# Layer 0's first squares summed on VectorE, pieces of the weight splits moved, and two expert tiles begun 64 bytes later

## The reference

```python
def rmsnorm(t, g):
    tf = t.astype(jnp.float32)
    y = tf * lax.rsqrt(jnp.mean(tf * tf, axis=-1, keepdims=True) + EPS) * g.astype(jnp.float32)
    return y.astype(t.dtype)
...
    rq = axial_rotary(heads(xs[4], RET_HEADS).astype(f32), *rope)
    rk = axial_rotary(heads(xs[5], RET_HEADS).astype(f32), *rope) * HEAD_DIM ** -0.5
...
    for e in range(N_EXPERTS):
        out = out + combine[:, e:e + 1].astype(t.dtype) * swiglu(t, w_gate[e], w_up[e], w_down[e])
```

## Time and profile before

| | |
|---|---|
| median of 3 runs | 2854.11 us (2850.2 to 2856.61) |
| the profiled execution | 2855.72 us, of which its span is 2853.9 us (1.8 us lie around it) |
| mean granted TensorE clock | 0.959 of 2.4 GHz |
| busy: PE, PEld | 2691.5 us (94%), 2267.1 us (79%) |
| busy: DVE, ACT | 1815.8 us (64%), 1462.7 us (51%) |
| chain that ended last | PE 85%, DVE 8%, ACT 4%, issue 2%, DMA 1% |
| experts | about from 1830 to 2829 us of the span |

### The profile page before, as it was taken

One profiled execution on the slowest core, in us unless ns is written; L12 is line 12 of the kernel. 1 busy time (PEld: TensorE's weight loads), 2 busy tenths in 40 slices (PEclk: granted clock), 3 DMA queues, 4 the chain that ended last, 5 costly groups with the idle time before them and its releaser, 6 DMA issues.

```text
span 2853.9 us, 38902 instructions
## 1 busy us (share of the span) xinstructions
PE 2691.5 (94%) x15426; PEld 2267.1 (79%) x15426; DVE 1815.8 (64%) x1907; ACT 1462.7 (51%) x1624; POOL 29.8 (1%) x40
## 2 busy tenths in 40 slices
PE   6999889999898999889899998899999999999998
PEld 3875568888796899877789986788888888888887
DVE  3224655553535676673355554688888888888887
ACT  3226333332335455532144444577777777777775
POOL 0001000000002000000000000000000000000000
PEclk8999999999999999996899999899999999999998
DMA  7546412322231444320034441599999999999996
GB/s 292 195 164 261 181 59 89 117 78 109 81 126 52 182 167 154 148 89 1 1 136 180 172 153 60 213 362 339 364 344 339 367 340 362 344 364 343 344 357 245
DMA packets 84359, 590.43 MB, mean 207 GB/s; under 512 B 9616, under 2 KB 10000, under 8 KB 19472
## 3 DMA queue, kind: packets, MB, share of 16 engines
q1 hardware_dynamic: 82800, 576.79, 54.5%
q10 hardware_dynamic: 1440, 11.93, 1.1%
HBM read 587.63 MB, written 1.05 MB: 206 GB/s over the span
## 4 chain that ended last, share of the span: by engine, by line
PE 85%; DVE 8%; ACT 4%; issue 2%; DMA 1%; DVEq 0%; POOL 0%; ACTq 0%; SPq 0%; POOLq 0%
PE banks L469 23%; PE banks L470 22%; PE banks L471 22%; PE banks L475 16%; DVE ring_rounded L531 2%; ACT ring_rounded L521 1%; DMA ring<-in_stream 1%; PE banks L2860 1%; PE banks L906 1%; DVE rstd L815 0%; ACT scratch L983 0%; DVE aT L2257 0%; DVE activations L1418 0%; DVE nmax L949 0%; DVE hT L1583 0%
## 5 line engine op out<-in xcount | busy, mean ns | idle before, releaser
L531 DVE TENSOR_TENSOR ring_rounded<-ring,ring_rounded 128x2048 fp32r<-128x2048 f32 (+4 forms) x168 | 339.6, 2023 | 455.1 <-ACT ring_rounded L521 454.1
L470 PE MATMUL banks<-aT_rounded,ring_rounded 128*128 128x256 f32 (+1 forms) x1632 | 532.0, 326 | 0.0
L470 PE MATMUL banks<-ring_rounded,activations_rounded 128*128 128x512 f32 x1344 | 527.5, 392 | 0.0
L521 ACT ACTIVATE ring_rounded<-ring 128x2048 fp32r<-128x2048 f32 (+4 forms) x168 | 284.7, 1696 | 395.1 <-PE banks L471 386.7
L469 PE MATMUL banks<-aT_rounded,ring_rounded 128*128 128x256 f32 (+2 forms) x1120 | 338.3, 302 | 24.6 <-DVE aT_rounded L840 12.5
L470 PEld LDWEIGHTS banks<-aT_rounded,ring_rounded 128*128 128x128 f32 x1632 | 317.4, 195 | 24.3 <-issue 0.7
L471 PE MATMUL banks<-aT_rounded,ring_rounded 128*128 128x256 f32 (+2 forms) x1120 | 335.7, 300 | 0.0
L470 PEld LDWEIGHTS banks<-ring_rounded,activations_rounded 128*128 128x128 f32 x1344 | 252.7, 188 | 52.3
L3034 DVE TENSOR_TENSOR ring_rounded<-ring,tables_rounded 128x2048 fp32r<-128x2048 f32 x112 | 253.4, 2286 | 24.1 <-ACT tables_rounded L2952 23.9
L2952 ACT ACTIVATE tables_rounded<-ring 128x2048 fp32r<-128x2048 f32 x112 | 214.9, 1920 | 94.4 <-DMA ring<-in_stream 88.8
L469 PE MATMUL banks<-activations_rounded,ring_rounded 128*128 128x512 f32 (+1 forms) x724 | 247.9, 342 | 14.8 <-DVE aT_rounded L845 7.1
(11 more groups left out here) (333 smaller groups left out, 4796.5 us busy)
## 6 DMA issues: line engine op xcount, KB each, us to landing
ring<-in_stream SPq DMA_DIRECT2D x501, 1024.0 KB, 5.4
ring<-in_stream SPq DMA_DIRECT2D x32, 704.0 KB, 5.4
ring<-in_stream SPq DMA_DIRECT2D x28, 768.0 KB, 6.1
activations<-in_rpb ACTq DMA_DIRECT2D x2, 1536.0 KB, 6.3
ring<-in_stream SPq DMA_DIRECT2D x6, 512.0 KB, 5.1
tables<-in_tab_b ACTq DMA_DIRECT2D x1, 2436.0 KB, 8.6
tables<-in_tab_a ACTq DMA_DIRECT2D x1, 2304.0 KB, 9.0
hT<-in_h ACTq DMA_DIRECT2D x1, 2048.0 KB, 15.7
```

The lines of the kernel that those rows point to most:

```text
L470: pe.matmul(out, exact(upper), exact(w_lower), start=False, stop=False)
L521: act.activation(exact(upper), w, ACT.Copy).then_inc(g.s["act_pieces"], 1)
L531: dve.tensor_tensor(exact(w), w, rounded(upper), ALU.subtract).then_inc(g.s["dve_pieces"], 1)
```

## The change

It has five parts.

1. Start: norm ("n1", 0) is gathered on DVE like the others (blocks 1 to 6), and PE sums only blocks 6 and 7. ACT copies modulation rows 1 before it takes the root (`then`), and rows 2 and 3 before it issues the late tables.
2. Splits at the start: one piece is split ahead of the first norm and one within it, instead of two ahead.
3. The rotary on DVE stands before the last weight piece of the projection, in both layers (`rotate_first_dve`).
4. Layer 0 after retention: ACT makes one weight piece before the last block of the attended values. In norm ("n2", 0) the gathers stand behind the additions, PE sums from block 5 on, and the DVE's weight piece of m = 6 goes behind m = 7. In norm ("n1", 1) ACT's weight piece moves from the end to before the third square.
5. The two expert tiles in `tables` begin 16 floats (64 bytes) later.

```diff
 def first_sum(key):
-    if key in (("n1", 0), "last"):
+    if key == "last":
         return 0
-    return KD - 3 if key in (("n1", 1), ("n2", 1), "ffn0", "ffn1") else KD - 2
+    return KD - 3 if key in (("n1", 1), ("n2", 0), ("n2", 1), "ffn0", "ffn1") else KD - 2
 def is_gathered(key):
-    return key not in (("n1", 0), "last")
+    return key != "last"
...
     upper_act(g, act, end)
+    then()
     act.wait_ge(g.s["pe_norm"], g.at("summed", key, KD - 1))
...
 def proj_dve(g, dve, l):
     dve.wait_ge(g.const_in["tab_a"], 16)
     for name in IN_ORDER:
+        if name == IN_ORDER[-1]:
+            rotate_first_dve(g, dve, l)
         lower_dve(g, dve, 1 if name in (IN_ORDER[0], IN_ORDER[-1]) else 2)
...
-    for name in ("rq", "rk"):
-        for j in range(3):
...
     if l == 0:
+        upper_act(g, act, 1)
         out_upper_act(g, act, 7)
-        upper_act(g, act, 2)
+        upper_act(g, act, 1)
...
-... g.tabs[:, 1536:1536 + UNIT], g.tabs[:, 3584:3584 + UNIT],
+... g.tabs[:, 1552:1552 + UNIT], g.tabs[:, 3600:3600 + UNIT],
...
-        squares_act(g, e, ("n1", 0), g.hT, T2, None)
+        squares_act(g, e, ("n1", 0), g.hT, T2, None, then=lambda: mod_act(g, e, 0, 1))
+        for i in range(2, MOD_FIRST):
+            mod_act(g, e, 0, i)
         consts_act(g, e, False)
-        for i in range(1, MOD_FIRST):
-            mod_act(g, e, 0, i)
...
+        for k in range(1, KD - 1):
+            gather_dve(g, e, ("n1", 0), T2, k)
         rstd_dve(g, e, ("n1", 0), T2)
...
             if l == 0:
-                upper_act(g, e, 2)
+                upper_act(g, e, 1)
             e.wait_ge(*g.moment(("gain", l, 0)))
-            split_act(g, e, n1, T2, lambda k, s: g.mod[:, l, k, s:s + 1], g.n1_upper, l)
+            split_act(g, e, n1, T2, lambda k, s: g.mod[:, l, k, s:s + 1], g.n1_upper, 1)
...
         if l == 0:
-            only("dve", add_dve, "wo", l, T, lambda m, s: g.mod[:, l, 16 + m, s:s + 1], n2, lambda m: {0: 2, 6: 1}.get(m, 0))
+            only("dve", add_dve, "wo", l, T, lambda m, s: g.mod[:, l, 16 + m, s:s + 1], n2, lambda m: 2 * int(m == 0),
+                 lambda m: int(m == KD - 1), False)
...
-            squares_act(g, e, after, g.hT, T, lambda k: ("free", ("dn", l, k)), split_ahead_1 if l else lambda k: 0, 1 - l)
+            squares_act(g, e, after, g.hT, T, lambda k: ("free", ("dn", l, k)), split_ahead_1 if l else lambda k: int(k == 2))
```

More of the change, by code:

```diff
@@ L675, in first_sum, with squares_act @@
 def first_sum(key):
-    if key in (("n1", 0), "last"):
+    if key == "last":
         return 0
-    return KD - 3 if key in (("n1", 1), ("n2", 1), "ffn0", "ffn1") else KD - 2
+    return KD - 3 if key in (("n1", 1), ("n2", 0), ("n2", 1), "ffn0", "ffn1") else KD - 2
 def is_gathered(key):
-    return key not in (("n1", 0), "last")
-def squares_act(g, act, key, src, T, ready, pieces=lambda k: 0, end=0):
+    return key != "last"
+def squares_act(g, act, key, src, T, ready, pieces=lambda k: 0, end=0, then=lambda: None):
     for k in range(KD):
@@ L1067, in proj_act, with rotate_first_dve @@
             mod_act(g, act, l, MOD_FIRST + IN_ORDER.index(name))
+def rotate_first_dve(g, dve, l):
+    for name in ("rq", "rk"):
+        for j in range(3):
+            x = g.m1[name][:, j, 0:L]
+            dve.wait_ge(g.s["pe_projection"], g.at("mm", "swap", name, l, j))
+            dve.tensor_tensor(g.tmp[:, 4096:4096 + L], g.bank(("swap", name, l, j))[:, 0:L], g.tab("rot_sin"), ALU.mult).then_inc(g.s["dve_projection"], 1)
+            g.count("dve_projection", ("free", ("swap", name, l, j)))
+            dve.tensor_tensor(x, x, g.tab("rot_cos"), ALU.mult).then_inc(g.s["dve_projection"], 1)
+            g.count("dve_projection")
+            dve.wait_ge(g.s["dve_projection"], g.so_far("dve_projection"))
+            dve.tensor_tensor(x, x, g.tmp[:, 4096:4096 + L], ALU.add).then_inc(g.s["dve_projection"], 1)
+            g.count("dve_projection", ("rotated", name, l, j))
+            dve.wait_ge(g.s["dve_projection"], g.so_far("dve_projection"))
 def proj_dve(g, dve, l):
@@ L1815, in second_places @@
     g.units = [flat[:, UNIT * i:UNIT * i + UNIT] for i in range(EXPERT_RING)]
-    g.upper = [flat[:, UNIT * EXPERT_RING:UNIT * EXPERT_RING + UNIT], g.tabs[:, 1536:1536 + UNIT], g.tabs[:, 3584:3584 + UNIT],
+    g.upper = [flat[:, UNIT * EXPERT_RING:UNIT * EXPERT_RING + UNIT], g.tabs[:, 1552:1552 + UNIT], g.tabs[:, 3600:3600 + UNIT],
                wide[:, 0:UNIT], wide[:, UNIT:2 * UNIT], t[:, 2560:2560 + UNIT]]
@@ L3324, in first_block @@
             if l == 0:
-                upper_act(g, e, 2)
+                upper_act(g, e, 1)
             e.wait_ge(*g.moment(("gain", l, 0)))
-            split_act(g, e, n1, T2, lambda k, s: g.mod[:, l, k, s:s + 1], g.n1_upper, l)
+            split_act(g, e, n1, T2, lambda k, s: g.mod[:, l, k, s:s + 1], g.n1_upper, 1)
         if kind == "dve":
             if l == 0:
-                lower_dve(g, e, 2)
+                lower_dve(g, e, 1)
             e.wait_ge(*g.moment(("gain", l, 0)))
             norm_dve(g, e, n1, g.hT, T2, lambda k, s: g.gain[:, l, 0, k, s:s + 1], lambda k, s: g.mod[:, l, k, s:s + 1],
-                     None, g.n1_upper, l)
+                     None, g.n1_upper, 1)
         only("act", bias_act, l)
```

## The result

The changed kernel took **2821.57 us** (median of 4 runs, 2821.16 to 2823.66), the kernel before 2855.36 (4 runs, 2850.2 to 2858.29) beside it: a ratio of 0.9888, 95% interval 0.9876 to 0.99, or 34 us less. A second series gave 2825.19 (5 runs, 2821.01 to 2832.36) against 2852.35 (18 runs), a ratio of 0.991 (0.9895 to 0.9926), or 27 us less. The forecast was 2829, from a sum of 26.4 us, with a range of 2821 to 2840. Both medians lie in the range. The sum was nearer to the second series than to the first, and the experiments show why: up to 13 us of these kernels' time hang on the moments at which the granted clock falls, and no part of the change was made to set those.

What follows compares the result with a forecast made beforehand. PE was taken as the bound nearly everywhere, so only shortening its idle or slow time counted. Terms 6.7 + 6.3 - 1.2 + 3.7 + 0.8 + 10.1 = 26.4 us, off 2855.7, gave 2829 us, range 2821 to 2840.

Steps and rivals of the forecast that it cites:

- start: From kernel start to first projection matmul: fewer PE sums, shorter waits and a moved weight piece save 6.7 us, bounds 4 and 9.5.
- rotary, layer 0: End of layer 0's projection: rotating before the weight piece removes PE's 4.59 us wait and low clock, saving 6.3 us.
- rotary, layer 1: Layer 1's gate: PE waits for the weight piece until 863.0, losing 1.2 us; bounds 0 and 3.
- ("n2", 0): Layer 0's second norm: reordered gathers, additions and weight piece bring the reciprocal earlier, saving 3.7 us; bounds 2 and 4.
- ("n1", 1): Layer 1's first norm: moving ACT's piece lets the reciprocal follow the root directly, saving 0.8 us; bounds 0 and 0.8.
- expert tiles: In the experts, starting the two `tables` tiles 64 bytes later makes their units fast, saving 10.1 us; bounds 0 and 12.3.
- only the root: Start, behind the sums: PE no longer waits for the copy of modulation rows 1, only the root; 0.75 us less.
- The piece: Start, last modulation sum to first projection matmul: one DVE piece moves into the norm, saving 0.7 us.
- Rival 3: Start gives nothing: modulation runs at 1.2 GHz without the sums beside it and gathers are late; 2836 us, chance 0.05.
- ACT's early piece: In layer 0's retention: saves nothing, as PE's next wait is for the second piece.
- Rival 1: Experts: the tiles' start doesn't matter, the two are slow for another reason; 2839 us, chance 0.11.
- H1: Experts, later theory from the forecast's reading: moving-to-stationary distance modulo 512 counts, 256 is slow; test should save some 5 us.

Runs made afterwards that it cites:

- part4_only: Kernel before with part 4 alone (norms ("n2", 0) and ("n1", 1), ACT's early piece in the retention): 2849.85 us, ratio 0.9987.
- start_only: Kernel before with parts 1 and 2 alone (first norm gathered on DVE, one weight piece ahead of it): 2842.83 us, ratio 0.9956.
- again: The changed kernel run once more, nothing altered, in a second series: five runs, 2821.01 to 2832.36 us, median 2825.19.
- rotary_l0: Changed kernel with the rotary ahead of the last weight piece in layer 0 only, layer 1 in its old order: 2821.75 us.
- tiles_only: Kernel before with part 5 alone (the two expert tiles in `tables` 64 bytes later): 2842.95 us, ratio 0.9964.
- mixed_l1: Changed kernel with layer 1's query tiles rotated ahead of the last weight piece, key tiles behind it: 2836.71 us, in a second series 2838.0.
- sweep_a: Changed kernel with expert tiles in `tables` at 464 and 576 bytes beyond a multiple of 1024, `scratch` meant at 448; no time clearly given.
- sweep_b: Changed kernel with expert tiles in `tables` at 480 and 960 bytes beyond a multiple of 1024, `scratch` meant at 192; no time clearly given.
- starts_c: A kernel whose change and time the text given does not state under this name.
- stationary_64: Changed kernel with the experts' stationary tiles (xg, hT2) 64 bytes later: 2855.08 us, beside the changed kernel's 2825.19.

## Why the prediction was right, point by point

| term of the sum | predicted | shown | by |
|---|---|---|---|
| start | 6.7 | 10.4 at the first projection matmul (8.3 against part4_only's old start) | changed, start_only |
| rotary, layer 0 | 6.3 | 6.3 (130 to 200) | changed, again, rotary_l0 |
| rotary, layer 1 | -1.2 | -3.2 | changed against rotary_l0 |
| ("n2", 0) | 3.7 | 3.6 at the reciprocal | part4_only, changed, again |
| ("n1", 1) | 0.8 | 0.7 | the same |
| expert tiles | 10.1 | 10.4 | tiles_only |
| changes of expert | 0 | 2.1 (0.5 and 1.8 with the old tiles: start_only, part4_only) | changed |
| the clock elsewhere | 0 | about 4, and 1 in the other profile | changed, again |

*Start: the term was mis-sized, at a step of its own.* The end of the two sums at 25.5 (25.35) and the wait for "only the root" (0.7 less) were right. "Bounds: 4 (the modulation runs at the low clock throughout, as it has less PE work beside it) and 9.5 (at the high clock throughout)": the condition of the upper one came true (the clock was 1.00 throughout the modulation), the term went 0.9 us beyond it, and I had taken the middle by leaving the modulation as it was. The row 34.40 to 41.20 is the 2.9 us. The piece gave 1.3, not 0.7, because the issue of the two transfers ran beside ACT's last copy instead of behind it, as ACT's timeline shows:

```profile
32.78 0.60 ACT L637 ACTIVATE mod_rows<-banks 128x512 f32<-128x512 f32 x1 [3.03 <-PE banks L475]
32.79 0.35 ACTq L500 DMA_DIRECT2D tables<-in_tab_a  x1
33.18 0.45 ACTq L500 DMA_DIRECT2D pool_w<-in_pool_w  x1
33.67 1.48 ACT L521 ACTIVATE ring_rounded<-ring 128x1536 fp32r<-128x1536 f32 x1 [0.29 <-issue]
```

The first projection matmul was forecast near 43.5 and came at 39.8. Rival 3, the opposite of this, was wrong by its premise that fewer sums leave the clock low: after the sums, the clock next falls at 36 to 40 us in all ten profiles with the new start, behind the modulation, and in all four with the old one at 33 to 34.5, within it.

*Rotary, layer 0.* Right in size. Its "bounds 3 and 6.3" held; 1.5 us of it went again by 230 us, because the clock was at 0.50 for 6.8 us (204.1 to 210.9) where the kernel before had 3.4 (225.5 to 228.9).

*Rotary, layer 1.* The wait was forecast as one for the piece, of 2 to 3 us, and was 2.89 us. "1.2 us lost; bounds 0 and 3 (a low clock after the wait)": the wait cost 1.3 us, about as summed, and the clock, which I had left to the bound, the rest: with it the term went 0.2 beyond the bound. After 2.89 us of idle the clock fell for 3.4 us, in all six profiles with this order; with 1.58 us before (and in rotary_l0) it did not.

*Norms.* Right, ACT's early piece included.

*Expert tiles: the right number by a wrong step.* The prices by unit held to 0.3 us in 10. Rival 1 fell, since only the start moved. The rule that spoke against this term (the Trainium skill, "SBUF — State Buffer", "Who interferes with whom") has no place for an operand's start in the time, and by it the sum would have been 16.3; units of 2.80 that become 2.72 with 64 bytes don't agree with that. But the argument "704 is also 64 beyond a multiple of 128, so alignment to 128 is not the cause" was false, for `scratch` lay at 896, not where I had counted it. The count gave distances of 0, 256 and 320 bytes modulo 512, which led to H1, and H1 fell. That the 64 bytes were right for `tables` under each reading was luck.

*The clock, which the sum left out.* I counted 1.7 us of it at the gate and nothing elsewhere. In the first profile it gave 3.1 us at the wait for modulation and 1.4 at 349, and gave back 1.5 at 225, besides the 2.9 within the start. Against layer 1's 2.0, the start (3.7), the changes of expert (2.1) and the clock (about 4) all went beyond the sum the same way: the first median lies 0.6 us inside the range, and that it does is in part luck. The kernel's spread after the change (2821 to 2832) is wider than the bounds of any term but the expert tiles.

## What to carry to other kernels

Where a matmul of the same shape has two prices by buffer, read the true addresses of both operands from the compiled program before looking for a rule, and put them where the fast ones lie: here 64 bytes were worth 10 us, and 64 bytes the wrong way on the other operand cost 23. Moving an independent chain ahead of a piece paid where the piece had 8 us of matmuls before it was asked for, and cost where it had 4; there the order half and half left no wait. A gain that is clear in its own place may be gone at the end: compare the same matmul in two profiles along the whole program, and time a kernel with sparse PE stretches in more than one series.

## What the runs showed of the hardware

**Where operands begin.** A unit is twelve fp32r matmuls of 512 columns; what it takes above 2.72 us, by the bytes beyond a multiple of 256 at which its tiles begin:

| moving (`stationary` at 128) | 128 | 0 | 192 | 96 | 80 | 64 |
|---|---|---|---|---|---|---|
| above 2.72 us, ns | 0 | 27 | 41 | 67 | 79 | 76 to 94 |
| in the `aT` or `ring` unit behind, ns | 0 | not seen alone | 36 | not seen alone | not seen alone | 44 |

At 192 the split is 41 and 36 in 24 of 32 undisturbed units and 80 and 0 in the other 8, so the two units lose about 80 ns together. With the moving tiles at 128 and the stationary ones at 192 it is 80 ns for every unit. All that is fast has both at 128. Two readings are left: each operand has a toll of its own unless it begins at 128 beyond a multiple of 256, or the difference of the two starts modulo 256 counts (0 fast; 64, 128 and 192 slow, with 41, 27 and 76 to 94 ns). The second fits only roughly: slow units in a row cost 80 ns each with the stationary tiles moved, but 76, 94 and 44 behind them in the kernel before. Moving both by 64 would tell them apart; that wasn't tried. A slow unit shows it as starts of matmuls up to 239 ns apart instead of 227.

**The clock and the moment.** A wait of about 2 us may or may not bring PE from 2.4 to 1.2 GHz, and its length did not decide it: at the wait for modulation the clock fell with 1.93, 1.99 and 2.23 us and did not with 1.95, 2.10 and 2.26. And once at 1.2 GHz in a stretch of small matmuls, it may stay there: 3, 7 or 48 us at the attention near 1720, with PE then busy 43.5 of 44 us. The long stretch came in all five profiles of kernels that were 22 us or more ahead of before at 1700 (mixed_l1 twice, sweep_a, sweep_b, starts_c), and in none of the nine others, before among them; it costs about 13 us. Those kernels do nothing else in that stretch than the changed one does; what differs is where in it the clock falls. Counted from the first matmul behind the softmax wait of 1.98 or 1.99 us, the clock fell after 1.65 to 1.70 us in seven profiles and was low for 6.8, after 1.82 and 1.84 in two (changed_again, stationary_64) and was low for 3.4, and after 2.05 or 2.06 in the five with 47.8. So the length goes with the moment of the fall within the same work, and edits elsewhere shift that moment. Why a fall 0.4 us later lasts seven times as long stays open, and no run here set the moment on purpose.
